# Where x lies in SBUF: 64-byte line 1 instead of 2, modulo 8, in a two-block transformer kernel

## What is computed

```python
# layer A: q,k,v,gate from x @ w_in; chunkwise retention; norm; silu gate; @ w_out
return (o * jax.nn.silu(gate)) @ w_out
# layer B: latent q and kv, rope, causal softmax over 16 heads, silu gate, @ w_out
o = _causal_block_attention(q_nope, q_rope, k_nope, k_rope, v).reshape(b, s, WIDTH_B)
# second block
x = x + jnp.concatenate([a, b], axis=-1) @ w_out[l]
h = rmsnorm(x, norm_mlp_g[l])
x = x + jnp.square(jax.nn.relu(h @ w_up[l])) @ w_down[l]
return rmsnorm(x, final_g)
```

## The kernel before

| buffer | before | after |
|---|---|---|
| stage, whi, wlo, whi_a, wlo_a, vs_a, pool_hi, wp_hi, wp_lo | 2 | 2 |
| xhi, xlo, s_hi2, s_lo2, comb, stage2, vs_b, xres, grow, ident | 2 | 1 |
| cols / stat / mv / small / eps | 2 / 3 / 6 / 6.5 / 0.5 | the same |
| oT, bT, mixT, hid, h_tok, nv_hi, nv_lo | 1 | 1 |
| c, ql, qk_pair, ar, br, nz, cr, dr | 2 | 2 |
| wkr_hi / wkr_lo / pool_lo | 6 / 2 / 3.5 | the same |

## Time and profile before

### The profile page before, as it was taken

One profiled execution on the slowest core, in us unless ns is written; L12 is line 12 of the kernel. 1 busy time (PEld: TensorE's weight loads), 2 busy tenths in 40 slices (PEclk: granted clock), 3 DMA queues, 4 the chain that ended last, 5 costly groups with the idle time before them and its releaser, 6 DMA issues.

```text
span 1385.1 us, 19133 instructions
## 1 busy us (share of the span) xinstructions
PE 1367.3 (99%) x7308; PEld 1182.2 (85%) x7308; DVE 1008.2 (73%) x1671; ACT 745.7 (54%) x1197; POOL 305.8 (22%) x161
## 2 busy tenths in 40 slices
PE   8999999999999999999999999999999999999998
PEld 7788888888888888888888888778888999998887
DVE  7979687889933755554555479936868887889895
ACT  5453535466544443344334446648956556576554
POOL 2050414110134444333433310025213000000000
PEclk9999999999999999999999999999999999999999
DMA  7458575475367988965796556354122675455552
GB/s 268 165 177 232 196 203 174 141 280 203 135 191 216 320 206 236 279 185 150 227 280 183 164 213 260 140 191 127 53 85 76 176 210 151 144 180 213 191 192 103
DMA packets 53898, 260.37 MB, mean 188 GB/s; under 512 B 5568, under 2 KB 10304, under 8 KB 28224
## 3 DMA queue, kind: packets, MB, share of 16 engines
q1 hardware_dynamic: 37152, 163.04, 33.6%
q0 software_dynamic: 5760, 41.95, 15.4%
q10 hardware_dynamic: 10912, 54.40, 10.9%
HBM read 252.03 MB, written 91.23 MB: 248 GB/s over the span
## 4 chain that ended last, share of the span: by engine, by line
PE 80%; DVE 13%; DMA 3%; ACT 2%; issue 1%; SPq 0%; POOL 0%; DVEq 0%; ACTq 0%; POOLq 0%
PE bank L614 21%; PE bank L616 21%; PE bank L615 21%; PE bank L1336 6%; PE bank L1398 3%; PE bank L1287 3%; DVE wlo L2291 3%; PE bank L1315 1%; DVE wlo_a L2291 1%; DMA v_spill<-v_tok 1%; DMA cols<-in_cols 1%; DMA stage<-in_w 1%; DMA stage<-tsum 1%; DVE ar_lo L2291 1%; DVE xres L2469 1%
## 5 line engine op out<-in xcount | busy, mean ns | idle before, releaser
L793 POOL TENSOR_TENSOR wlo<-stage,whi 128x1024 fp32r<-128x1024 f32 (+2 forms) x68 | 169.1, 2512 | 436.6 <-ACT whi L1618 350.3
L1621 ACT ACTIVATE whi<-stage 128x1024 fp32r<-128x1024 f32 (+2 forms) x155 | 148.2, 1002 | 111.1 <-PE bank L616 92.3
L2291 DVE TENSOR_TENSOR wlo<-stage,whi 128x1024 fp32r<-128x1024 f32 (+1 forms) x133 | 152.8, 1177 | 13.9 <-ACT whi L1621 13.8
L614 PE MATMUL bank<-xhi,whi 128*128 128x256 f32 (+1 forms) x300 | 98.6, 329 | 1.6 <-POOL wlo L929 1.2
L616 PE MATMUL bank<-xhi,wlo 128*128 128x256 f32 (+1 forms) x300 | 98.5, 328 | 0.0
L615 PE MATMUL bank<-xlo,whi 128*128 128x256 f32 (+1 forms) x300 | 98.5, 328 | 0.0
L1618 ACT ACTIVATE whi<-stage 128x1024 fp32r<-128x1024 f32 (+2 forms) x74 | 76.1, 1079 | 19.7 <-issue 14.6
L2291 DVE TENSOR_TENSOR wlo_a<-stage,whi_a 128x1024 fp32r<-128x1024 f32 (+1 forms) x60 | 71.6, 1217 | 15.2 <-ACT whi_a L1621 15.2
L614 PE MATMUL bank<-whi,xhi 128*128 128x512 f32 (+1 forms) x204 | 78.3, 384 | 2.1 <-DVE wlo L2291 1.2
L616 PE MATMUL bank<-whi,xlo 128*128 128x512 f32 (+1 forms) x204 | 77.3, 379 | 0.0
L615 PE MATMUL bank<-wlo,xhi 128*128 128x512 f32 (+1 forms) x204 | 77.2, 378 | 0.0
(11 more groups left out here) (499 smaller groups left out, 4332.8 us busy)
## 6 DMA issues: line engine op xcount, KB each, us to landing
stage<-in_w SPq DMA_DIRECT2D x71, 1024.0 KB, 5.0
tsum<-in_w ACTq DMA_DIRECT2D x32, 1024.0 KB, 12.2
stage<-tsum SPq DMA_DIRECT2D x32, 1024.0 KB, 4.8
tsum<-in_w POOLq DMA_DIRECT2D x16, 1024.0 KB, 10.0
tsum<-tsum POOLq DMA_DIRECT2D x16, 1024.0 KB, 9.9
stage<-in_w SPq DMA_DIRECT2D x8, 1152.0 KB, 6.9
usum<-in_w POOLq DMA_DIRECT2D x8, 1024.0 KB, 10.0
stage<-usum SPq DMA_DIRECT2D x32, 256.0 KB, 3.9
```

Of the source, the lines that this page charges most:

```text
L614: pe.matmul(dst, a_hi, b_hi, start=start, stop=False, skip_group_check=onto)
L793: pool.tensor_tensor(lo[:, r], stage[p % 2][:, r], hi[:, r].bitcast(F32), ALU.subtract).then_inc(w_lo, 1)
L1621: act.activation(dst, src, ACT.Copy, scale=scale).then_inc(signal, 1)
L2291: dve.tensor_tensor(dst, src, hi.bitcast(F32), ALU.subtract).then_inc(signal, 1)
```

## The change

Five small buffers (14, 48, 8, 32 and 4 fp32 numbers per partition, 448 bytes with rounding, that is 7 lines) are reserved ahead of xhi instead of behind the identity matrix. All buffers between the two places begin 7 lines later, which is line 1 modulo 8 instead of 2; those in front and behind keep their addresses. Instructions, their order on every engine, waits and transfers are the same.

```diff
         gap("gap_a", 256)
+        cols = sb("cols", [P, COLS])
+        stat = sb("stat", [P, TT, 2, 6])
+        mv = sb("mv", [P, TT, 2])
+        small = sb("small", [P, 4, 8])
+        eps = sb("eps", [P, 4])
         with ExitStack() as h:
             s_hi2 = sb("s_hi2", [P, PK, HALF], F32R, h)
             s_lo2 = sb("s_lo2", [P, PK, HALF], F32R, h)
...
         xres = sb("xres", [P, TT, DM])
         grow = sb("grow", [P, DM])
         ident = sb("ident", [P, P])
-        cols = sb("cols", [P, COLS])
-        stat = sb("stat", [P, TT, 2, 6])
-        mv = sb("mv", [P, TT, 2])
-        small = sb("small", [P, 4, 8])
-        eps = sb("eps", [P, 4])
         first_layer = ctx.enter_context(ExitStack())
```

## The result

| | before | changed |
|---|---|---|
| median of the runs | 1386.05 us (8 runs, 1385.06 to 1386.9) | 1388.53 us (8 runs, 1387.46 to 1391.58) |
| span of the profiled execution | 1385.1 us | 1385.4 us |

The ratio is 1.0021, 95% interval 1.0012 to 1.0029. The change is slower by 2.5 us; the forecast was 8.5 us slower, with a range of 1380 to 1404. The direction was right, the size was off by a factor of more than three. The two profiled executions differ by only 0.3 us. The one of before was a long one for its kernel: in 21 later ones the span was 1383.0 to 1385.5 us, median 1384.2, and the time about 2 us over it, not the 0.8 that the forecast names (the 0.8 does not enter its sum, which starts from the median time). The changed one was the shortest of its eight.

What follows compares the result with a forecast made beforehand. TensorE's matmul pace was taken as the bound: (1008 + 768) x-moving matmuls x 4.8 ns = 8.5 us, 1224 stationary ones and others 0; 1385.9 + 8.5 = 1394.4 us, range 1380 to 1404.

Steps and rivals of the forecast that it cites:

- The bound: Whole kernel: TensorE is busy 99% of the span, so time is the number of matmuls times the distance between starts.
- Price for x moving, 512 columns: 1008 matmuls with x moving over 512 columns: +4.8 ns each, 231.4 instead of 226.6 ns between starts.
- the disturbed one after pool_lo: Before the change, seven starts from pool_lo's matmul on were 231.4 ns apart; an operand staying off might keep this pace.
- 256 columns: 768 matmuls with x moving over 256 columns: +4.8 ns each, with ends 0 and +8.4.
- the 13.3 ns on top: Start distance beyond the columns' own time: 120.0 ns is 106.7 + 13.3 at 256 columns, about the same at 512.
- x stationary: 1224 matmuls of 512 columns with x, vs_b or s_hi2 stationary: 0 taken, with ends +4.8 and -6.7 ns.
- The nv rows: Six 256-column matmuls with nv at line 1 as stationary operand start 113.3 ns apart, not 120: no cost there.
- Others: Other engines that read or write the moved buffers, the five small buffers and all other matmuls: cost 0.
- Like before: Rival for the whole kernel: the steady pace settles again at another phase, time 1385.9; chance 0.30.
- cancelling mixture at 1386.2: Case of unchanged time: moving operands pay 8.5 us and stationary ones gain 8.2.
- Both pay: Rival: the 1224 stationary-operand matmuls pay 4.8 ns too, 5.9 us more, time 1400.3; chance 0.15.
- Faster: Rival: unlike start lines avoid a collision of stream and weight load, 6.7 ns x 1224 = 8.2 us, time 1377.7; chance 0.20.

Runs made afterwards that it cites:

- The third version: Kernel before, with x, dr and s2u one line before their partners in the up product and c one line further on: 1378.64 us, ratio 0.9951.

## Why the prediction was wrong

**The bound.** Right: TensorE's pace is the bound, and a few ns on 3000 matmuls are visible in the time.

**Price for x moving, 512 columns.** Right. Forecast 4.8 ns, 4.8 us on 1008 matmuls; measured 5.2 ns, 5.5 us on 1056. That a lasting distance would keep a pace like the disturbed one after pool_lo was right. That the size fits so well is part luck. The steady stages pay 6 ns (226.5 to 232.5), and the groups of line 1398 only 1 to 2 ns, because their pace was no steady 226.6 before either (398 in the earlier trace rows), which the forecast passed over. pool_lo stands for half a line, which measures +5.7 on the mean, while whole lines give 2.6 to 5.2 by their distance, and nothing at four lines.

**256 columns.** This is the step that failed: "I take the same +4.8 as for 512, since the 13.3 ns on top is the same in both." Measured is -5.9 ns, -4.5 us instead of +3.7. The 13.3 ns on top are the same at D = 0, but they don't react in the same way. It moves the sum by 8.2 us, more than the 5.2 us between the forecast (8.5) and the measured change of pace (3.3); the stationary operands, below, take part of it back. Why a distance costs at 512 columns and gains at 256 stays open. A row that showed 256 columns at 113.3 instead of 120 was there, and I used it for the stationary operand alone. It would not have given the size either: nv stands at D = +1, where x moving shows 118, and reads its columns in two runs.

**x stationary.** A second, smaller miss: forecast 0, measured 2.1 ns, 2.6 us. The nv rows, of 256 columns, were carried to 512, where the same distance costs.

**Others.** Right: other matmuls and engines did not change; the 512-column groups of c, ar, br and dr kept their 389 to 391.

**Rivals.** *Like before* named a cancelling mixture at 1386.2, in which stationary operands give back what moving ones pay. Things do cancel, but by width: moving and stationary operands both pay at 512 columns, and it is the narrow stage that gives back. *Both pay* is true at 512 columns (8.1 us), but not in the sum. *Faster* had the right size for a gain, 120 to 113.3 ns, but it came at 256 columns, where x moves; x stationary, at 512 columns, paid. Its reason, a collision because both start on the same line, is not borne out: at 512 columns an unlike pair pays. The Trainium skill ("SBUF — State Buffer", section "Who interferes with whom") calls TensorE's two reads, of the moving operand and of the weights, independent, and says that PE never waits on anyone. No run here tests that between engines. But it can't be read as "the two start addresses don't matter to each other": eight placements with the same instructions cover 1385.7 to 1395.1 us. What happens inside, a collision of the two reads or something else, no run here shows; only the dependence on the distance is shown.

## What to carry to other kernels

In a kernel like this one, where each matmul has its own weight load and streams 512 columns of fp32r, try moving and stationary operand a multiple of 256 bytes apart first (0 and 256 were the best here), and read the distance between starts, not the busy share: PE was 99% busy at every placement. At 256 columns a moving operand one line (64 bytes) before the stationary one was faster here, so measure narrow and wide matmuls apart before carrying a price from one to the other. And when a cost is a sum over kinds, look whether one of the rows that argue "no cost" is of another kind than the one it is used for.

## Not expected of the hardware

- The pace depends on the distance of the start addresses of the two operands modulo 256 bytes, up to 7 ns of 227 at 512 columns by the means of the groups; a shift of all operands together by one line changed nothing (ratio 0.9998).
- Half a line off costs both kinds 6 ns and 9 us in the whole kernel.
- With all pairs at D = -1, 256-column matmuls have two lasting paces, 113.3 and 117.8 ns, and can change from one to the other within an execution, at a late start.
- Three of the traces with the same wait of 1.2 us before the up product had 3.4 us at the lower clock behind it, some 1.4 us longer; the others had none there.
- The third version, 1378.64 us, is faster than before and after (7.0 us less than before in its comparison).
